# Hybrid NSA + S5 block on one core: own places for the compression weights, another order of powers and flattened blocks, diagonals that normalise the probabilities inside their transposes, and a tail that goes token tile by token tile

## The reference, cut to what matters

```python
h = rmsnorm(x, norm_g)                        # x: (512, 1024) float32
proj = h @ w_in                               # q | kc vc ksl vsl kwi vwi | gl | gate_nsa | u | gate_s5 | mg
k_cmp, v_cmp = compress(kc, ...), compress(vc, ...)   # gelu(flat @ w1) @ w2, w1: (2048, 256), for K and for V
# attention, 8 heads in 2 groups: compressed, selected and window branch, each
p = masked_softmax(q @ k.T * scale, mask)     # e / max(sum(e), 1e-30)
o = p @ v
o_nsa = g0 * o_cmp + g1 * o_sel + g2 * o_win  # g = sigmoid(gl), one per token, head and branch
y = s5_scan(u, ...)                           # complex diagonal recurrence over the 512 tokens
branch_a = (o_nsa * silu(gate_nsa)) @ w_proj_nsa
branch_b = (glu(gelu(y)) * silu(gate_s5)) @ w_proj_s5
x = x + (sigmoid(mga) * branch_a + sigmoid(mgb) * branch_b) @ w_out
return rmsnorm(x, final_g)
```

## Time and profile before

| | |
|---|---|
| time, median of 3 runs | 471.16 us (469.15 to 473.84) |
| profiled execution | 476.43 us, its span 474.4 us |
| PE busy | 431.0 us, 91% of the span |
| DVE, ACT, POOL busy | 290.3, 201.2, 154.3 us |
| mean granted TensorE clock | 0.971 |

### The profile page before, as it was taken

How to read it: one execution, slowest core, us unless ns; L and a number is a source line. 1 busy time by engine, 2 the same in 40 slices (tenths; PEclk the granted TensorE clock), 3 DMA queues, 4 the chain that set the end, 5 groups by cost and what they waited for, 6 DMA issues and landing times.

```text
span 474.4 us, 7326 instructions
## 1 busy us (share of the span) xinstructions
PE 431.0 (91%) x2811; PEld 349.4 (74%) x2811; DVE 290.3 (61%) x645; ACT 201.2 (42%) x396; POOL 154.3 (33%) x78
## 2 busy tenths in 40 slices
PE   0999999979597998969998999999999999999991
PEld 0888888869375795646665677888888888899991
DVE  1666889999999545898999786134153070162334
ACT  5742778712125245697654642222322222233323
POOL 0342442431123401131314125544445444454420
PEclk9999999998898978999999999999999999999997
DMA  9954961221748227110101101564333334322104
GB/s 248 252 118 117 163 166 44 70 81 33 233 132 175 61 51 169 39 44 2 46 0 47 29 18 44 173 226 110 109 90 92 88 91 118 104 90 90 46 0 177
DMA packets 72738, 47.27 MB, mean 100 GB/s; under 512 B 21144, under 2 KB 69728, under 8 KB 72672
## 3 DMA queue, kind: packets, MB, share of 16 engines
q1 hardware_dynamic: 71520, 46.74, 37.6%
q10 hardware_dynamic: 1184, 0.07, 0.2%
HBM read 42.61 MB, written 4.19 MB: 99 GB/s over the span
## 4 chain that ended last, share of the span: by engine, by line
PE 60%; DVE 16%; ACT 5%; issue 3%; DMA 3%; POOL 1%; SPq 0%; DVEq 0%; ACTq 0%
PE bank L885 16%; PE bank L887 16%; PE bank L886 16%; DMA raw<-in_w_in 3%; PE bank L1154 3%; PE bank L1172 2%; PE bank L1193 2%; DVE bank L1271 2%; DVE prob L1607 2%; DVE pwt L1271 1%; DVE prob L1627 1%; PE bank L1108 1%; POOL w_lo L610 1%; DVE X L1271 1%; PE bank L1132 1%
## 5 line engine op out<-in xcount | busy, mean ns | idle before, releaser
L610 POOL TENSOR_TENSOR w_lo<-raw,w_hi 128x1024 fp32r<-128x1024 f32 (+2 forms) x57 | 137.2, 2406 | 258.3 <-ACT w_hi L638 258.3
L885 PE MATMUL bank<-hT_lo,w_hi 128*128 128x512 f32 x288 | 116.9, 406 | 6.3 <-POOL w_lo L610 6.2
L886 PE MATMUL bank<-hT_hi,w_lo 128*128 128x512 f32 x288 | 114.0, 396 | 0.0
L887 PE MATMUL bank<-hT_hi,w_hi 128*128 128x512 f32 x288 | 113.9, 396 | 0.0
L638 ACT ACTIVATE w_hi<-raw 128x1024 fp32r<-128x1024 f32 (+2 forms) x57 | 59.5, 1043 | 99.2 <-PE bank L887 78.3
L885 PEld LDWEIGHTS bank<-hT_lo,w_hi 128*128 128x128 f32 x288 | 55.1, 191 | 20.5 <-POOL w_lo L610 7.1
L887 PEld LDWEIGHTS bank<-hT_hi,w_hi 128*128 128x128 f32 x288 | 55.2, 192 | 12.0
L886 PEld LDWEIGHTS bank<-hT_hi,w_lo 128*128 128x128 f32 x288 | 55.1, 191 | 10.7
L830 ACT ACTIVATE prob<-prob,nmax 128x128 f32<-128x128 f32 (+2 forms) x64 | 35.3, 552 | 24.6 <-DVE nmax L1607 24.6
L886 PE MATMUL bank<-w_hi,m_lo 128*128 128x256 f32 x128 | 36.2, 283 | 0.0
L887 PE MATMUL bank<-w_hi,m_hi 128*128 128x256 f32 x128 | 36.2, 283 | 0.0
(11 more groups left out here) (211 smaller groups left out, 737.8 us busy)
## 6 DMA issues: line engine op xcount, KB each, us to landing
raw<-in_w_in SPq DMA_DIRECT2D x28, 512.0 KB, 3.9
raw<-in_w_in SPq DMA_DIRECT2D x16, 256.0 KB, 3.7
raw<-in_w_out SPq DMA_DIRECT2D x8, 512.0 KB, 3.4
x_sb<-in_x SPq DMA_DIRECT2D x4, 512.0 KB, 5.6
raw<-in_cmp_w_k SPq DMA_DIRECT2D x4, 512.0 KB, 4.0
raw<-in_cmp_w_v SPq DMA_DIRECT2D x4, 512.0 KB, 5.1
raw<-in_w_proj_s SPq DMA_DIRECT2D x4, 512.0 KB, 3.4
raw<-in_w_proj_nsa SPq DMA_DIRECT2D x8, 256.0 KB, 4.1
```

The source lines that it names most:

```text
L610: nc.gpsimd.tensor_tensor(view(w_lo, j % NSPLIT, dims), w, view(w_hi, j % NSPLIT, dims).bitcast(F32), ALU.subtract).then_inc(lo_done, 1)
L885: nc.tensor.matmul(dst, w[0], x[1], start=first, stop=False, skip_group_check=True)
L886: nc.tensor.matmul(dst, w[1], x[0], start=False, stop=False, skip_group_check=True)
L887: return nc.tensor.matmul(dst, w[0], x[0], start=False, stop=last, skip_group_check=True)
```

## The change

1. **Compression weights in own places.** They leave the raw ring. SP loads quarter i of both into `w1_even` or `w1_odd`, behind the blocks ksl, vc, gs3 and gn0 in its queue. gs2 and gs3 are each cut in two halves, which stand between the small steps of the compression. gn0 moves from bank 1 to bank 7.
2. **Powers and flats.** One doubling in `powers` takes 4 operations instead of 6, the first table is made before the C matrices instead of after them, and rotation and flattening stand one run step earlier.
3. **Diagonals.** DVE no longer multiplies the probabilities. It makes only the reciprocal; POOL multiplies the identity by reciprocal and gate, one 128 x 128 diagonal for each query tile and group; TensorE multiplies by the diagonal where it transposed by the identity. DVE copies both groups' transposed probabilities. POOL's low parts are put between the diagonals.
4. **Tail.** w_out's first 512 channels are four blocks `wa{n}` of two contraction tiles, with one bank for each token tile; then channels 512 to 767 as before; then 768 to 1023 one token tile after another, for which the low and high part of the last block get a third place. The root, the scaling and the stores go by token tile, each tile's two halves stored apart (256 KB each).

```diff
-    for i, n in enumerate(("val1", "val2", "gs0", "gs1")):
-        b += [(n, 1), (f"w1k{i}", 0), (f"w1v{i}", 0)]
...
-    b += [(f"wo{q}_{h}", 1) for q in range(4) for h in range(2)]
+    b += [(f"wa{n}", 1) for n in range(4)]
+    b += [(f"wo{q}_{h}", 1) for q in (2, 3) for h in range(2)]
...
-    use("gn0", 1)
+    use("gn0", 7)
...
+            def compression_weights(i):
+                if i == 0:
+                    wait_fill(sp, f"xT{KT - 1}")
+                elif i == 1:
+                    wait_fill(sp, "KR")
+                else:
+                    sp.wait_ge(compressed, i - 1)
+                for r, n in enumerate("kv"):
+                    w = a["cmp_w1_" + n][0].rearrange("(kt p) n -> p kt n", p=P)[:, 4 * i:4 * i + 4, :]
+                    sp.dma_start((w1_even, w1_odd)[i % 2][:, r], w).then_inc(w1_in[i % 2], 16)
...
+            def diagonals(w):
+                r, b, tiles = steps[w]
+                if w >= 3:
+                    wait_fill(pl, f"PT1_{w - 3}")
+                pl.wait_ge(coef_done, w + 1)
+                for g in range(GROUPS):
+                    for k, i in enumerate(tiles):
+                        nc.gpsimd.tensor_scalar(diag[w % 3][:, g, k, :], ident[:, :], coef[:, w % 4, g, k:k + 1],
+                                                gate[:, i, HPG * g + r, 1 + b:2 + b], ALU.mult, ALU.mult).then_inc(diag_done, 1)
...
-            channel_major("gs2", "gs2")
+            channel_major("gs2", "gs2", kts=(0, 4))
...
-                            ins = nc.tensor.transpose(bk(job)[:, col:col + P], prob[:, w % 4, g, c + P * kt:c + P * kt + P],
-                                                      ident[:, :])
+                            ins = nc.tensor.matmul(bk(job)[:, col:col + P], prob[:, w % 4, g, c + P * kt:c + P * kt + P],
+                                                   diag[w % 3][:, g, tiles.index(i), :], start=True, stop=True, skip_group_check=True)
...
+            w = weights("wo3_0"), weights("wo3_1")
+            pe.wait_ge(r_done, NT)
+            for i in range(NT):
+                open_bank(pe, f"W3_{i}")
+                for kt in range(KT):
+                    ins = mm3(bk(f"W3_{i}")[:, 0:256], merged(kt, i), [v[:, kt % 4, :] for v in w[kt // 4]], kt == 0, kt == KT - 1)
+                fill(ins, f"W3_{i}")
...
-                    tt(t0, dst[:, 0, 0:n], fr, MUL)
-                    tt(t1, dst[:, 1, 0:n], fi, MUL)
-                    tt(dst[:, 0, n:2 * n], t0, t1, SUB)
-                    tt(t0, dst[:, 0, 0:n], fi, MUL)
-                    tt(t1, dst[:, 1, 0:n], fr, MUL)
-                    tt(dst[:, 1, n:2 * n], t0, t1, ADD)
+                    tt(by_re, dst[:, :, 0:n], fr, MUL)
+                    tt(by_im, dst[:, :, 0:n], fi, MUL)
+                    tt(dst[:, 0, n:2 * n], by_re[:, 0], by_im[:, 1], SUB)
+                    tt(dst[:, 1, n:2 * n], by_im[:, 0], by_re[:, 1], ADD)
...
-                link(V.reciprocal(coef[:, s % 4, :, 0:n], den[:, s % 4, :, 0:n]))
-                for g in range(GROUPS):
-                    for k, (i, c) in enumerate(tile_offsets(tiles)):
-                        pi = prob[:, s % 4, g, c:c + P * (i + 1)]
-                        V.tensor_scalar(pi, pi, coef[:, s % 4, g, k:k + 1], gate[:, i, HPG * g + r, 1 + b:2 + b], MUL, MUL)\
-                         .then_inc(p_done, 1)
+                V.reciprocal(coef[:, s % 4, :, 0:n], den[:, s % 4, :, 0:n]).then_inc(coef_done, 1)
...
+            for i in range(NT):
+                residual(f"W3_{i}", slice(i, i + 1), slice(768, 1024))
+                ve.wait_ge(fin_sq, 2 * NT + i + 1)
+                link(V.tensor_reduce(rms[:, 0, i:i + 1], ssq4[:, i:i + 1, 0:3], AX_X, ALU.add))
+                variance(fin_var, i, i + 1)
+                times_gain(slice(i, i + 1), slice(768, 1024))
+                ve.wait_ge(rg_done, 4 + i)
+                inverse_root(fin_sqrt, i + 1, i, i + 1, root_done)
+                V.tensor_scalar(r_sb[:, i, 0:512], r_sb[:, i, 0:512], rms[:, 3, i:i + 1], None, MUL).then_inc(y_ready[i], 1)
```

More of the change, by code:

```diff
@@ L573, in _ @@
                     u_to_scratch()
+                if name in ("ksl", "vc", "gs3", "gn0"):
+                    compression_weights(("ksl", "vc", "gs3", "gn0").index(name))
                 if name == "q3":
@@ L891, in weights @@
                 pe.wait_ge(lo_done, split_at[name] + 1)
-                dims = wdims(name)
-                return [view(w, slot(name), dims) for w in (w_hi, w_lo)]
+                return split_views(name)
             def hT(kt, cols=slice(0, T)):
@@ L1046, in compress @@
                     open_bank(pe, "H")
[L1047 to L1051 removed]
+                pe.wait_ge(w1_in[i % 2], 32 * (i // 2 + 1))
                 for kk in range(4):
@@ L1079, in _ @@
             fill(ins, "HT")
-            channel_major("gs3", "gs3")
+            channel_major("gs2", "gs2", kts=(4, KT))
             pe.wait_ge(cmp_in, 16 * 2)
```

341 lines of the change are left out of this document (189 added, 152 removed).

## The result

The changed kernel takes **470.43 us** (median of 20 runs, 469.72 to 471.76). The kernel before, run beside it, took 474.49 us (median of 20 runs, 468.18 to 476.14 and one of 716.19). The ratio is 0.9946, with a 95% interval of 0.9924 to 0.9969. On a second chip (the first experiment) it was 470.88 against 474.42 us, ratio 0.9929 [0.9903, 0.9954]. So the change is faster, but by little: 0.5 to 0.7% by the ratios, which is 2.6 to 3.4 us, and 3.5 to 4.1 us by the medians. The forecast was 464.9 us against a median of 471.16, that is 6.3 us or 1.3% less.

The account below looks back on a forecast made before the run. TensorE was taken to bound the attention, VectorE close behind, and the last stage, with waits in the stage before them. -14.1 + 10.8 - 3.0 = -6.3 us against the 471.16 us median gave 464.9 us, range 457 to 475.

Parts of the forecast that it names:

- Up to the attention: Stages ahead of the attention: ring and powers changes let the attention start 14.1 us sooner, bounds 9 and 17.
- the second rotation: VectorE's scan chain: 1.2 us taken back because it reads two SBUF operands and moves into a low part's time.
- The bounds: VectorE's scan: bounds of 0 and 7 us around the forecast that it ends 3.5 us sooner.
- The run steps, flattenings and carries are the same work in another order: nothing: VectorE's scan chain: reordering these was counted as no change in time.
- The attention: Attention stage: 10.8 us longer, 18.6 us of extra records less waits and clock regained; bounds 8.5 and 23.
- The tail: Last stage: 3.0 us shorter, from wider matmuls and from residual, scaling and stores by tile; bounds -1 and -4.5.
- the Sum: Whole kernel: -14.1 + 10.8 - 3.0 = -6.3 us, taken against the median of 471.16 to give 464.9 us.
- The scan does not move: Rival ahead of the attention: collisions with GpSimd's low parts eat the scan's 3.5 us; 469.9 us, chance 0.15.
- A factor of four: Rival in the attention: a float32 product costs four times a transpose; 55.7 instead of 18.6 us, kernel 502, chance 0.03.
- The second pass costs more than a slot: Rival in the attention: unhidden loads of the stationary probabilities make 160 products cost 42 us more; kernel 488.5, chance 0.10.
- GpSimd the bound: Rival in the attention: at 2 us a diagonal GpSimd needs 156.7 us; kernel 500.6, chance 0.05.
- mostly hidden: Rival in the attention: TensorE's busy time holds overlaps, so +5 instead of +10.8 us; kernel 459.1, chance 0.07.

Follow-up runs that it names:

- the first experiment: The changed kernel again, unaltered, on the same chip as the other variants, beside the kernel before: 470.88 us, ratio 0.9929.
- e5: The kernel before with only the compression weights in own places, gn0 in bank 7 and gs2 and gs3 in halves: 467.05 us, ratio 0.9825.
- e7: The changed kernel with the old powers and the old order of rotation, flattenings and run steps: 474.49 us, ratio 0.9994 to the kernel before.
- e2: The changed kernel without the diagonals, with the transposes, VectorE multiplications and ScalarE copies of before: 458.91 us, ratio 0.9683.
- e4: The kernel before with its 160 transposes made true float32 products with the identity, no diagonals: 488.16 us, ratio 1.0297.
- e3: The kernel before with the diagonals alone: 482.94 us, ratio 1.0152.
- e6: The kernel before with the tail by tiles alone: 471.44 us, ratio 0.9924.
- the last two experiments: e9 and e10, run beside a third set of runs of the kernel before (median 474.94 us): 473.15 and 453.34 us.
- e10: The kernel of e8 with the compressed probabilities' transposes moved behind the second step's scores and a piece of gn1, in banks 5 and 6: 453.34 us.
- e8: The kernel of e2 with gn0's matmuls ahead of TensorE's wait for the scan and the work around it reordered: 457.18 us, ratio 0.9623.
- e9: The kernel of e7 with the copy of the scan's end states done by ScalarE, not VectorE: 473.15 us, ratio 0.9976.

## Why the prediction was wrong: the mechanisms held, the sum did not

**Up to the attention (14.1 us forecast, 13.4 found).** Right, step by step: the three waits gone, one wait of 7.2 us for the scan (6 to 10 said), S5 outputs at 155.02 (near 154 said). The scan moved by 2.7 us, not 3.5. What stood ahead of the run steps came out as forecast: they begin at 86.81 instead of 91.71 us, 4.9 sooner (some 5 said). The power operation of the earlier trace rows lost its collision, though a pair of 2.70 us at 65.73 took its place beside the same low part. The loss is behind the first run step, where 1.2 us were taken back for the second rotation:

```profile
86.81 1.43 DVE L1350 TENSOR_TENSOR bank<-X,bank 128x512 f32<-128x512 f32 x2 [0.45 <-ACT X L714]
90.72 1.67 DVE L1350 TENSOR_TENSOR bank<-k_swap,rope 128x512 f32<-128x512 f32 x1 [0.85 <-ACT k_swap L765]
```

The rotation now waits 0.85 us for ScalarE, and its first product takes 1.67 us instead of 0.70, since it starts within a low part (89.44 to 91.84). With 0.3 us in a product at 106.23 and 0.1 in the copy, 4.9 becomes 2.7. The bounds held it. "The run steps, flattenings and carries are the same work in another order: nothing" missed more. The new order brings flat_k ahead of the next projection, which had waited 2.7 us for it; and the order, with the clock, decides how much of the copy falls into a low part (it took 0.51 us in the change, 1.25 in e5, 2.31 in e7).

**The attention (10.8 us forecast, 11.7 found, 12.7 against e2).** The kind of each item was right: 160 x 0.116 = 18.6 us of records forecast, 19.1 found between e2 and the change, and e4 shows that they are the whole price. What comes back was put at 7.8 us (6.6 of waits and 2.2 of clock, less 1.0), and 7.4 was found (19.1 - 11.7). The largest error in it is the clock's: 2.2 us were taken, but e2, at a clock of 1.00, is busy for 102.16 us where before was busy for 103.63, 1.5 less. Whether this clock is owed to the diagonals stays open. The profiled kernels with 320 records have 1.00 in the attention, e3 and e4 too, which keep all of before's waits ahead of it; of those with transposes e2 has 1.00, the kernel before 0.98 and e5 0.97. GpSimd's diagonals took 0.45 to 0.48 us each on average, 0.43 was estimated, and were hidden as forecast.

**The tail (-3.0 us forecast, -3.4 found, -3.4 alone in e6).** Right: -0.7 in the matmuls and last block, and 7.0 us behind the last matmul where 7.3 was forecast.

**The step that failed is the Sum**, where the text goes from one execution to a median: "it lies 5 us above the median of 471.16, and against that median I forecast 464.9 us". The saving of 6.3 us was read from the waits and clocks of one execution and then taken off another number in full. Three things went wrong there, two of them in the saving and one in the base.

- *The terms.* Between the two profiled executions the saving came out at 5.3 us, 1.0 less than the sum: the scan (0.8 us) and the attention (0.9), against 0.4 more from the tail, with smaller differences.
- *The execution.* The 476.43 us from which they were read lie 1.9 us above the median of its 20 runs, the changed kernel's 471.09 only 0.7 above its own. That is another 1.3 us: 6.3 forecast, 5.3 between profiles, 4.1 between medians (2.6 by the ratio).
- *The base.* The kernel before took 474.49, 474.42, 474.80 and 474.94 us in four larger sets (20, 12, 17 and 17 runs); the three runs of 471.16 were 3.3 us too low. That alone moves 464.9 to 468.2, and the 1.0 and the 1.3 us make up the rest of the way to 470.4. It is why the number was missed, and not why the saving was.

What the clock does to before's time is seen in its 17 runs beside the last two experiments: 469.7 us at a mean clock of 0.983, and 473.6 to 476.7 at 0.971 to 0.975. The traces show where such time can lie. Before, e3, e4 and e6 run the same program up to the attention and begin it at 183.09, 181.56, 183.04 and 182.06 us. From 100 to 110 us, around the same 2.68 us wait for flat_k, the kernel before (first row) and e3 (second) differ, and from 186 to 190 us the kernel before has a clock of 0.76 (third) where the other three have 1.00, although all four wait 2.14 us ahead of their first scores:

```profile
100.00:110.00 10.00, 7.32 (x46) 7.09 (x45) 9.50 (x21) 1.58 (x2) 2.41 (x2) 0.83 0.11 29
100.00:110.00 10.00, 7.32 (x56) 7.10 (x56) 9.50 (x22) 1.29 (x2) 3.40 (x2) 1.00 0.11 29
186.00:190.00 4.00, 4.00 (x14) 2.34 (x13) 2.85 (x14) 2.75 (x11) 0.00 (x0) 0.76 0.88 300
```

So the same wait is followed by the low clock in one execution and not in another. Why stays open, and so does which stretch sets the 1.9 us, since only one execution of before was profiled. That fewer waits mean less spread isn't shown either. The change and e10, with few waits, lie within 2.1 us over their runs; but e4, with all of before's waits ahead of the attention, lies within 1.2, and e5, without the ring's, within 4.5.

**The rivals.** "The scan does not move" gave 469.9 us, the nearest number, for a wrong reason: the scan moved by 2.7 us. "A factor of four" fell. Rows show two records for a true product and one for a transpose, at the same pace, so the factor is two. The Trainium skill's factor of four in favour of the transpose mode for float32 ("TensorE: Matmul & The Clock Gate", section "Terms") is not what these 128 x 128 tiles show. "The second pass costs more than a slot", "GpSimd the bound" and "mostly hidden" fell too: 0.120 us each, 57 us of GpSimd beside 122, and 12.7 us of 19.1 not hidden.

**What the whole change amounts to.** Ring, powers and tail are worth 15.5 us together. By themselves the ring gave 7.8 and the tail 3.4, and part 2 is worth 3 to 4 inside the change. The diagonals give up 12.0 of these 15.5. They take work from VectorE, which had 17 to 19 us to spare in the attention, and add it to TensorE, which had 7.

## What to carry to other kernels

Moving work to the bounding engine costs its whole slot time and returns at most that engine's waits; measure it by a variant that lacks this one part, not by the change as a whole, since three good parts can cover a bad one. A saving that is the difference of two large terms inherits both their errors and that of the base: with a spread of 5 us between runs, three of them do not fix a median to within a saving of 6. When an engine waits for a late chain, moving independent work ahead of the wait pays only if what stands behind the chain on all engines is moved along (1.7 us in e8, 5.6 with e10).

## What the runs showed of the hardware

- A VectorE copy from SBUF to SBUF (128 x 480, float32) that starts within a GpSimd subtraction ends 0.27 us behind its end: 0.41 us alone, 0.51, 1.25 and 2.31 with the overlap. A product of two SBUF operands (the rotation's, 128 x 512) took 1.67 us where it started within a subtraction, and 0.70 in the kernel before. On ScalarE the same copy took 0.61 us beside a subtraction of GpSimd (e9). VectorE's scan operations with one operand in PSUM kept their 0.62 us beside the subtractions. The profile counts the stalled copy as busy.
- A float32 product of 128 x 128 by 128 is two records and occupies TensorE for twice a transpose of the same tile (0.118 and 0.116 us a record).
- TensorE had no work from 147.84 to 155.02 us in the changed kernel, and from 155 to 160 us its granted clock was 0.53 of full, so nearly all of these five microseconds were at 1.2 GHz. Eight of the U_sh matmuls took 0.70 us there. In e10, behind a wait of 1.7 us, eight took 0.45, and the clock was 1.00 from 150 to 160 us. The changed kernel's stretch (columns as in the earlier trace rows), then e10's row:

```profile
155.00:160.00 5.00, 4.98 (x100) 5.00 (x104) 4.74 (x12) 0.66 (x2) 0.00 (x0) 0.53 0.07 13
```

```profile
154.09 0.45 PE L1182 MATMUL bank<-U_sh,TT 64*64 64x128 f32 x8 [1.73 <-issue]
```

- GpSimd's product of a 128 x 128 identity with two per-partition scalars takes 0.45 us in the median, and 1.38 at most.
